# Differential attention of a diffusion backbone step: heads run as 72 equal rounds, transposed blocks split 4+4+1 over two working banks, small products in spare PSUM columns

## What is computed

```
p1 = softmax(einsum("bhqd,bhkd->bhqk", q1, k1) * scale)
p2 = softmax(einsum("bhqd,bhkd->bhqk", q2, k2) * scale)
o  = einsum("bhqk,bhkd->bhqd", p1 - lam * p2, v)
o  = rms_norm(o, subln_w) * (1.0 - lam_init)
```

## Time and profile before

| what | value |
|---|---|
| median of three executions | 3567.09 us (3557.61 to 3573.65) |
| span of the profiled execution | 3560.5 us |
| TensorE busy in it | 3329.0 us (93%) |
| VectorE, ScalarE, GpSimd busy | 53%, 33%, 26% |
| mean granted TensorE clock | 0.968 |
| differential attention, from the last projection of head 0's v to the last out bank | 106.1 to 907.03 us |

### The profile page before, as it was taken

The page is one execution under the profiler, slowest core; times in us unless marked ns, Lnnn a source line. Parts: engine busy times, 40 slices in busy tenths (PEclk is TensorE's granted clock), DMA queues, the critical chain, the costliest instruction groups (busy, mean ns, idle before and its releaser), DMA issues. The chain is left out here.

```text
span 3560.5 us, 51583 instructions
## 1 busy us (share of the span) xinstructions
PE 3329.0 (93%) x20797; PEld 3075.1 (86%) x20797; DVE 1872.0 (53%) x2655; ACT 1185.3 (33%) x2106; POOL 939.9 (26%) x726
## 2 busy tenths in 40 slices
PE   5999999997989999999989999999899999999996
PEld 4777777786989999999978777777799999999996
DVE  4555565564165455555454555555326454555455
ACT  3344444444132121221133555555423111221212
POOL 1122222122333222322242112221143222322221
PEclk8999999997999999999999999999899999999998
DMA  6333333323211111111113111101331111111101
GB/s 244 99 97 106 105 105 104 110 67 129 89 45 56 37 41 35 41 50 44 36 53 72 33 26 35 29 20 35 110 93 61 36 42 35 41 53 41 35 30 60
DMA packets 206659, 229.78 MB, mean 65 GB/s; under 512 B 30564, under 2 KB 173533, under 8 KB 205341
## 3 DMA queue, kind: packets, MB, share of 16 engines
q1 hardware_dynamic: 186973, 162.69, 15.2%
q10 hardware_dynamic: 11664, 42.47, 3.5%
q0 software_dynamic: 7856, 22.29, 1.7%
HBM read 181.79 MB, written 31.98 MB: 60 GB/s over the span
## 5 line engine op out<-in xcount | busy, mean ns | idle before, releaser
L205 PE MATMUL psum<-Hh,wh 128*128 128x384 f32 x3360 | 1141.5, 340 | 33.8 <-ACT Hh L412 12.9
L207 PE MATMUL psum<-Hl,wh 128*128 128x384 f32 x3360 | 1130.4, 336 | 0.0
L206 PE MATMUL psum<-Hh,wl 128*128 128x384 f32 x3360 | 1130.3, 336 | 0.0
L311 DVE SCALAR_TENSOR_TENSOR x<-psum,mod,x 128x384 f32<-128x384 f32 (+2 forms) x768 | 377.0, 515 | 655.3 <-PE psum L207 610.5
L205 PEld LDWEIGHTS psum<-Hh,wh 128*128 128x128 f32 x3360 | 636.4, 189 | 44.9 <-issue 18.8
L206 PEld LDWEIGHTS psum<-Hh,wl 128*128 128x128 f32 x3360 | 636.2, 189 | 0.0
L207 PEld LDWEIGHTS psum<-Hl,wh 128*128 128x128 f32 x3360 | 636.1, 189 | 0.0
L851 POOL TENSOR_TENSOR wl<-wr,wh 128x1024 fp32r<-128x1024 f32 x88 | 219.6, 2496 | 987.9 <-ACT wh L769 987.9
L801 ACT ACTIVATE ff_u<-psum 128x768 f32<-128x768 f32 x88 | 71.6, 814 | 1110.5 <-PE psum L207 1110.5
L205 PE MATMUL psum<-ff_ah,ff_dh 128*128 128x384 f32 x1056 | 364.8, 345 | 29.4 <-POOL ff_al L874 20.7
L1002 DVE SCALAR_TENSOR_TENSOR ff_c<-ff_u,par,ff_c 128x1153 f32<-128x1153 f32 x176 | 377.3, 2144 | 15.8 <-DVE ff_c L999 5.2
(11 more groups left out here) (217 smaller groups left out, 4241.9 us busy)
## 6 DMA issues: line engine op xcount, KB each, us to landing
wr<-w_up SPq DMA_DIRECT2D x88, 512.0 KB, 3.9
ff_dr<-w_down SPq DMA_DIRECT2D x22, 1024.0 KB, 6.0
da_mw<-mod_w ACTq DMA_DIRECT2D x40, 512.0 KB, 3.9
wr<-mod_w ACTq DMA_DIRECT2D x40, 512.0 KB, 4.8
wr<-w_qkv_diff SPq DMA_DIRECT2D x24, 512.0 KB, 19.9
x<-x_save SPq DMA_DIRECT2D x16, 576.0 KB, 6.4
in_mw<-mod_w SPq DMA_DIRECT2D x8, 1024.0 KB, 12.3
Hh<-oh_save SPq DMA_DIRECT2D x14, 576.0 KB, 9.8
```

Source lines behind the costliest of these rows:

```text
L205: pe.matmul(out, w_hi, m_hi, start=start, stop=False)
L206: pe.matmul(out, w_lo, m_hi, start=False, stop=False)
L207: return pe.matmul(out, w_hi, m_lo, start=False, stop=stop)
L311: last = dve.scalar_tensor_tensor(g.x[:, m, lo:hi], g.PS[:, bank, lo - n * NB:hi - n * NB], g.mod[:, gate + m, cond:cond + 1], g.x[:, m, l ...
```

## The change

`Ring` gives way to `Turns`, with all uses of the phase in one list. Heads have no borders: the phase is a row of 72 rounds, round r = 9h + s computing the scores of tile s of head h and working off tile r - 2. All nine thirds of the next head's projections lie in rounds 0 to 8 (`PROJ`), M and MT in rounds 3 to 8 of a head, behind W. The 9 blocks of a tile are split as 4, 4 and 1, each in a working bank of its own (`blocks_of`; `rider` returns None). The first 4 blocks stand in front of the scores, together with ST, BC, ck and ko, which no longer use the working banks: they go to columns 384 and up of banks 0, 3, 4 and 5 (`spot`), after the exponentials of the tile before and ahead of the next scores. VectorE reads ST and BC out around the two maxima, and accumulates M after `combine`.

```diff
+    def turned_tile(r):
+        return at(r - 2) if r >= 2 else None
+    def weighted(r):
+        if r < 2:
+            return []
+        h, t = at(r - 2)
+        return [("PV", h, t // 2)] if t % 2 or t == QT else []
+    def means(r):
+        return [("ST",) + u[1:] for u in (weighted(r - 1) if r >= 1 else [])]
+    def spreads(r):
+        return [("BC",) + u[1:] for u in (weighted(r - 2) if r >= 2 else [])]
+    def in_front(r):
+        uses, tile = [], turned_tile(r)
+        if tile:
+            uses.append(("T",) + tile + (0,))
+        uses += means(r) + spreads(r)
+        if r < ROUNDS and at(r)[0] < LAST:
+            uses += {2: [("ck", at(r)[0] + 1)], 3: [("ko", at(r)[0] + 1)]}.get(at(r)[1], [])
+        return uses
+    def behind(r):
+        uses, tile = [], turned_tile(r)
+        if tile and tile[1] < QT:
+            uses.append(("T",) + tile + (1,))
+            if rider(r) is None:
+                uses.append(("T",) + tile + (2,))
+        if r >= ROUNDS:
+            return uses + weighted(r)
+        h, s = at(r)
+        if h < LAST:
+            uses.append(project_use(r))
+        uses += slice_uses(h, s) + weighted(r)
+        return uses + {1: [("vt", h, 0)], 2: [("vt", h, 1), ("vt", h, 2)]}.get(s, [])
+    def rider(r):
+        tile = turned_tile(r)
+        return None
+    def blocks_of(use):
+        t, i = use[2:]
+        return (0, 1) if t == QT else ((0, 4), (4, 4), (8, 1))[i]
+    def spot(use):
+        if use[0] == "ST":
+            return PS[:, 0, NB:NB + 2]
+        if use[0] == "BC":
+            n = PAIRS[use[2]][1]
+            if use[1] == LAST and use[2] >= 2:
+                return PS[:, 3, 0:n * P].rearrange("p (c q) -> p c q", c=n)
+            return PS[:, 3:3 + n, NB:NB + P]
+        return PS[:, {"ck": 5, "ko": 4}[use[0]], NB:NB + P]
...
+            for r in range(ROUNDS):
+                for use in in_front(r):
+                    if use[0] == "T":
+                        do(use, r)
+                scores_free(r)
+                for use in in_front(r):
+                    if use[0] != "T":
+                        do(use, r)
+                scores(r)
+                for use in behind(r):
+                    do(use, r)
...
+            def round_out(r):
+                for use in in_front(r) + behind(r):
+                    if use[0] == "T":
+                        tile_out(use)
+                if r < ROUNDS:
+                    softmax(r)
+                for use in in_front(r) + behind(r):
+                    if use[0] in ("ck", "ko"):
+                        keys_out(use)
+                    if use[0] == "W":
+                        project_out(use, rider(r))
+                    if use[0] == "vt":
+                        value_out(use)
+                    if use[0] == "PV":
+                        outputs(use)
...
+            for r in range(ROUNDS):
+                h, s = at(r)
+                round_out(r)
+                next_slice(r)
+                if h < LAST and s in (1, 4):
+                    w_hi(h + 1, W_HI_AT[s])
+                if h + 2 < HEADS and s == 7:
+                    w_hi(h + 2, "k")
...
+            for r in range(ROUNDS):
+                h, s = at(r)
+                for use in means(r):
+                    mean_square(use, r)
+                maximum(r, 0)
+                for use in spreads(r):
+                    normalise(use, r)
+                maximum(r, 1)
...
+                combine(r)
+                for use in slice_uses(h, s):
+                    accumulate(use)
```

More of the change, by code:

```diff
@@ L63, in rope_tables, with __init__, bank, done @@
     return np.concatenate([cos, cos], axis=0), np.concatenate([sin, sin], axis=0)
[L66 to L111, removed]
+class Turns:
+    def __init__(self, uses, own):
+        self.order, self.place, self.prior = {}, {}, {}
+        count, turns = {}, 0
+        for use in uses:
+            assert use not in self.order
+            self.order[use] = len(self.order)
+            if use[0] in own:
+                continue
+            place, turns = "AB"[turns % 2], turns + 1
+            self.place[use], self.prior[use] = place, count.get(place, 0)
+            count[place] = count.get(place, 0) + 1
+    def bank(self, use):
+        return {"A": WORK, "B": WORK + 1}[self.place[use]]
+    def done(self, use):
+        return self.order[use] + 1
+    def wait_free(self, eng, free, use):
+        if self.prior[use]:
+            eng.wait_ge(free[self.place[use]], self.prior[use])
+    def wait_read(self, eng, free, use):
+        eng.wait_ge(free[self.place[use]], self.prior[use] + 1)
 class Chain:
@@ L1261, in phase_diff_attention @@
     Y0 = 3
[L1265 to L1276, removed]
-        if ahead and s in (2, 3):
-            u += [("ck",) if s == 2 else ("ko",)]
-        u += [("BC", p) for p in BC_AT.get(s, [])]
-        return slice_uses(h, s) + u
@@ L1450, in next_slice, with outputs @@
-            def next_slice(ring, h, s):
-                m = PIECE.get((h.index, s))
+            def outputs(use):
+                h, p = use[1:]
+                n, i = PAIRS[p][1] * P, pair(h, p)
+                if i >= 2:
+                    act.wait_ge(b.y_d, i - 1)
+                act.wait_ge(b.full, ring.done(use))
+                act.activation(b.sq[:, i % 2, 0:n], PS[:, ring.bank(use), 0:n], ACT.Square)
+                act.activation(b.o[:, i % 2, 0:n], PS[:, ring.bank(use), 0:n], ACT.Copy).then_inc(free[ring.place[use]], 1)
@@ new lines, in _ @@
+            load_slice(act, 0, 0)
+            for (x, n), bank in AHEAD.items():
+                projected(("W", 0, x, n), PS[:, bank, :], b.ahead)
+            for use in FIRST:
+                if use[0] == "W":
+                    act.wait_ge(b.full, ring.done(use))
+                    projected(use, PS[:, ring.bank(use), :], free[ring.place[use]])
+                else:
+                    keys_out(use)
+                if use == ("W", 0, "k", 2):
+                    w_hi(0, "v")
+                if use == ("W", 0, "q", 2):
+                    w_hi(1, "k")
@@ new lines, in mean_square, with spread @@
+            def mean_square(use):
+                h, p = use[1:]
+                ring.wait_read(pe, free, ("PV", h, p))
+                for i in range(PAIRS[p][1]):
+                    last = pe.matmul(spot(use)[:, i:i + 1], b.sq[:, pair(h, p) % 2, i * P:(i + 1) * P], g.ones_v[:, :], start=True, stop=True)
+                last.then_inc(b.full, 1)
+            def spread(use):
+                h, p = use[1:]
+                pe.wait_ge(b.r_d, pair(h, p) + 1)
+                for i in range(PAIRS[p][1]):
+                    last = pe.matmul(spot(use)[:, i, :], b.r[:, p, i:i + 1].to_broadcast([P, P]), g.ident[:, :], start=True, stop=True)
+                last.then_inc(b.full, 1)
```

632 lines of the change are left out of this document (290 added, 342 removed).

## The result

| | before | changed |
|---|---|---|
| median (20 executions each) | 3563.11 us (3556.55 to 3573.68) | 3577.38 us (3572.49 to 3584.92) |
| ratio of the medians, 95% interval | | 1.0041 (1.0033 to 1.0049) |
| span of the profiled execution | 3560.5 us | 3579.2 us |
| first scores | 111.69 us | 112.47 us |
| head 0 (first scores to those of head 1) | 98.27 us | 94.86 us |

The account below looks back on a forecast made before the run. TensorE's own list bounds heads 1 to 6, so waits there count. Heads +9, MT +3.6, start +1 and last head -2 give +12 us on the span, 3572.5; with 6.6 to the median, 3579 us, range 3556 to 3600.

Parts of the forecast that it names:

- The call "same": Whole kernel: 3579 us, 0.3% above now, taken as not told from no change (about 0.5%, 18 us); chance 0.64.
- (a): Projection W waits for the copy of T1, whose bank it needs: 0.73 us, 8 times a head, 5.8 us.
- (b): ST ahead of scores waits for PV's readers: 0.45 us in rounds 4, 6, 8, 0.84 in round 1; 2.2 a head.
- (c): Values' transpositions (vt) take W's bank in rounds 1 and 2, waiting 0.4 us for its copy: 0.8 a head.
- (d): Short round 8: ScalarE issues two DMAs and splits a weight before copying T0; W starts about 0.7 us later.
- (f): PV waits for MT's bank, read late by VectorE: 2.0 us once, 0.4 twice; with W's bank waits, +3.6 us together.
- (g): Start: array idle 5.6 us before first scores, slow restart about 2.6, round 0 filled: +1 us (-3 to +4).
- (h): Last head without W: 17.7 us per pair of rounds, 102 us, 4.6 of it moved from before: -2 (-8 to +4).
- Rival 3: The clock falls once a head behind two waits close together: 7 x 2.6 = 18 us, 3597; chance 0.09.
- the prediction's own sign: Heads 1 to 6: the prediction is wrong if the clock there is under 1.00.
- Rival 1: W waits only 0.37 us: -20 us, 3559; if the last head's array also stays up, 3549; chance 0.13.
- Rival 2: VectorE accumulates M late behind rotation and `combine`, and T0 needs that bank: some 16 us, 3595; chance 0.13.

Follow-up runs that it names:

- The first experiment: Against the changed kernel, the ninth transposed block goes into the spare columns of the projection's bank: 3529.97 us, 0.9904 of before.
- the second profile: The changed kernel run once more, nothing altered, for another profile: 3570.92 us in one execution, span 3569.2 us.

## Why the prediction was right, and where it was wrong

The forecast was 3579; it came out at 3577.4, 0.41% above. The call "same" rested on the statement that a measurement can't tell some 0.5% from no change. With twenty executions it can: the interval is 0.33% to 0.49%. The mechanism is the one that was forecast, waits of W and ST in place of those at the borders, and its middle is well hit: 101.15 a head and 3.6 for MT are 610.5 us for six heads, against 611.0 and 607.0 in the two profiles. Point by point:

- **(a) T and W.** Forecast: W starts 1.37 us after T1. Measured: 1.34 to 1.43, nearly everywhere. What was off is the split of it: five blocks were given 0.64, so the wait was put at 0.73. Without the wait they take 0.52, and it is 0.82 to 0.91. For the sum that made no difference. The first experiment's expectation took the 0.6 to 0.7 of the rows instead, and that made most of its 11 us.
- **(b) ST.** The wait is there at 0.46, and 0.79 in round 1, as forecast, but it is worth 0.64 and 0.88. Three times 0.2 a head are 0.6 us too little.
- **(c)** holds: 0.45 once and 0.34 in the next round.
- **(d) ScalarE's queue in round 8** failed. The step was that two DMA issues and a weight split hold back the copies that W needs, by 0.7 us. The issues lie beside operations that were issued before them, and hold back only the split behind them, by 0.26:

```profile
503.20 0.38 ACT L1513 ACTIVATE da_sq<-psum 128x256 f32<-128x256 f32 x1 [4.65 <-PE psum L1669]
503.26 0.34 ACTq L1348 DMA_DIRECT2D da_mw<-mod_w  x1
503.48 0.38 ACT L1514 ACTIVATE da_o<-psum 128x256 f32<-128x256 f32 x1
503.62 0.46 ACTq L1349 DMA_DIRECT2D wr<-mod_w  x1
504.12 1.06 ACT L1454 ACTIVATE wh<-wr 128x1024 fp32r<-128x1024 f32 x1 [0.26 <-issue]
505.09 1.37 ACT L1476 ACTIVATE da_pt<-psum 128x512 f32<-128x512 f32 x3
```

  T0's copy does stand behind the split, but T1's follows on it without a gap, and W starts 1.35 us after T1 in the short round too: 0.7 was forecast on top, nothing came.
- **(f) MT.** Waits of 0.15, 1.81 and one of 0.56: 2.5 us, with 3.6 forecast; the long one was forecast at 2.0. The earlier trace rows was the right place to read it.
- **(g) Start.** The idle time is 6.58 us (5.6 forecast) and the restart slow, as said:

```profile
112.47 0.69 PE L1711 MATMUL psum<-da_nkh,da_nqh 64*128 64x384 f32 x2 [6.58 <-issue]
```

  Head 0 behind it takes 3.4 us less, so start and head 0 come to -2.6 (0.78 - 3.41). The forecast has +1 here, but it books under (h) the 4.6 us of work that leave head 0: -3.6 is to be set against the -2.6.
- **(h) Last head.** The -1.3 beside the forecast's -2 is luck. The stretch was forecast at 102 us, 2.9 above before; the -2 has the 4.6 of head 0 in it. It took 97.79, so this term was 4.2 too long. The four pairs of rounds, forecast at 17.7 each, took 16.5, 20.0, 16.9 and 16.8, together 70.1 in place of 70.8; T0 waits 3.87 and 2.85 us in the first two, for the copies of PV and of the values, and no term has these waits. The rest of the stretch, from the short tile's scores at 888.46 us on, took 27.7 where the forecast leaves 31.2; this is the part that it passed over with "fewer waits". The granted clock rose too, 0.91 in place of 0.81.
- **Unpriced: the border.** +3.3 us, shown above to be GpSimd's end. The forecast named the last head's end as "under out banks, with fewer waits", and did not ask which engine ends last there. The forecasts (g) and (h) together were 3.0 us too long, so these errors cancel.
- **Unpriced: the clock in round 8.** Rival 3 put a fall in each of seven heads at 2.6 us. It came in two heads of one profile and in none of the other, at 1.5 and 1.7 us. By the prediction's own sign, a clock under 1.00 in heads 1 to 6, the first profile (0.99) speaks against it and the second (1.00) does not. Its statement that the trace of before shows nothing between waits of 0.7 and 2.54 us was wrong: M waits up to 1.2 us for its load in heads 1 to 6 there, and the clock stays at 1.00. Windows of the changed kernel, around round 8 of head 4:

```profile
504.50:506.00 1.50, 1.44 (x12) 0.97 (x11) 0.91 (x4) 1.47 (x3) 0.74 (x1) 1.00 0.83 254
506.00:508.00 2.00, 1.71 (x7) 1.66 (x7) 2.00 (x1) 1.15 (x6) 2.00 (x2) 0.71 0.74 301
508.00:510.00 2.00, 2.00 (x8) 2.00 (x8) 1.90 (x4) 0.00 (x0) 0.81 (x1) 0.50 0.48 141
```

The phase from first scores to the next phase's start is thus 0.78 - 3.41 + 13.08 - 1.35 + 3.26 = 12.4 us longer with the two falls, and 9.9 in the second profile, without them. The forecast had 12, partly by cancelling errors. The remaining 6 us of the profiled spans' 18.7 lie in phases with the same code, 1.4 of them in the slow matmuls behind the border; in the second profile the other phases are 1 us shorter than before. Lastly, the step from span to median, 6.6 us, came from three executions; with twenty, the distance is 2.6. With that step the forecast would have been 3575, 2.3 us under the result.

Rival 1 (shorter waits) fell: the waits are longer than their rows. Its second part, a last head without restarts, came only in part (0.91, not 1.00). Rival 2 (VectorE late) fell: no matmul of T0 waited for it in heads 1 to 6. The reason given against rival 1, that a bank with four blocks can't be read sooner, held in every variant: W waited as long as the copy ahead of it ran past the work that lay between, with 1, 3 or 4 blocks there.

## What to carry to other kernels

Where uses take turns on two buffers, each waits until the buffer's last use has been read, and only the one use between hides that: a reading of 0.6 us wants a long use behind it, and the shortest use belongs where its own short reading is what must be hidden (4, 1, 4 rather than 4, 4, 1), or in a bank that is held anyway. Put work that waits for nobody (here M) between a product and the use that needs another engine's reading of it. A change with a gain and a loss inside can time as nearly nothing: take it apart, since here the rounds gained some 3 to 5 us, the new split lost 17, and a third place for the ninth block is worth 47 against that split. Where a phase ends in a barrier, ask for each engine when it ends, not only for the one that is busy; in this case the late one also cost TensorE its upper clock at the start of the next phase.

## What the runs showed that was not expected

- **A wait costs more than its idle time in the matmul rows.** 0.24 us more at W, 0.18 at ST, and all of it where the wait is under some 0.25 us. Over heads 1 to 6, taking W's waits away shortened the time by 607.01 - 571.01 = 36.0 us, of which 558.01 - 546.11 = 11.9 us was "busy" time of the same 3653 matmuls. The weight loads' busy time stayed, 470.90 and 469.72, and their idle time ahead of W (21.9 + 17.3 = 39.2 us in the first profile) is here the better measure of what can be won. The Trainium skill ("Perfetto Trace Analysis", Identifying the Most-Contended Engine) says that the busy share of matmuls is no good measure of how near a kernel is to its limit, because they are pipelined, and names the share of the peak arithmetic and the weight loads' busy share instead. These two windows agree: for the same work the matmuls' busy time fell by 11.9 us and the weight loads' by 1.2.
- **The clock can fall behind short waits.** In round 8 of some heads, where 0.48 us of short scores stand between the means and T1, W took 5.9 in place of 4.4 us at a granted 0.50, the 1.2 GHz level. The array had waited 0.46 us ahead of ST and some 0.35 ahead of W, with short products between. The full rounds, with waits of 0.46 and 0.67, kept 1.00 in every head. It was seen in the changed kernel (2 heads in one profile, none in the other), with T0 behind (3 heads) and with groups of 4, 1 and 4 (2); not once with the block in the spare columns (5 profiles), nor with the slice added up ahead, whose waits are those of the changed kernel. In a full round it came once, with groups of 3, behind PV's wait of 2.04 us for VectorE. Behind 1.81 us at the same place of the changed kernel it did not, nor behind 2.48 us there with groups of 4, 1 and 4 and with the block in the spare columns:

```profile
380.38 4.15 PE L1669 MATMUL psum<-da_pt,da_v 128*128 128x256 f32 x18 [2.48 <-DVE mod L445]
```

  So the length of the last wait alone does not decide it. That the waits of the short round cause the fall is likely from these counts, but with so few profiles it is not shown. The Trainium skill ("TensorE: Matmul & The Clock Gate", A second HAM failure mode: psum-queue depth-cycling) describes just such a fall behind brief idle times between groups; the traces agree with it in some of the short rounds and not in the full ones.
- **ScalarE's DMA issues run beside operations that were issued before them** (503.26 beside 503.20 above). The one operation behind the two issues started 0.26 us late, by its row; in this round W did not start later for it.
